# A 31-tap depthwise convolution: four channel tiles by 16-tap products through DRAM, two by 2-tap products, two on VectorE

## The reference, cut to what matters

```python
def conformer_conv(h, w_in, b_in, w_dw, b_dw, ln_g, ln_b, w_out, b_out):
    a, g = jnp.split(h @ w_in + b_in, 2, axis=-1)
    u = a * jax.nn.sigmoid(g)
    u = lax.conv_general_dilated(u, w_dw[:, None, :], window_strides=(1,),
        padding=[(CONV_WIDTH - 1, 0)], feature_group_count=D_MODEL) + b_dw   # width 31, per channel
    u = (u - mean(u)) * lax.rsqrt(var(u) + LN_EPS) * ln_g + ln_b             # over the channels
    return jax.nn.silu(u) @ w_out + b_out

def _rg_lru(...):
    a = jnp.exp(log_a)
    u = jnp.sqrt(-jnp.expm1(2.0 * log_a)) * (i * x)     # the recurrence's roots
    _, h = lax.associative_scan(_lin_combine, (a, u), axis=1)
```

## Time and profile before

| | |
|---|---|
| median of 3 runs | 2126.19 us (2125.86 to 2126.7) |
| the profiled execution | 2126.1 us, its span 2124.3 us |
| PE busy | 2084.4 us (98%) |
| PEld busy | 1861.9 us (88%) |
| DVE busy | 1596.5 us (75%) |
| ACT busy | 1230.8 us (58%) |
| POOL busy | 56.4 us (3%) |
| mean granted TensorE clock | 0.996 of full speed |

### The profile page before, as it was taken

The page is one execution under the profiler, slowest core; times in us unless marked ns, Lnnn a source line. Parts: engine busy times, 40 slices in busy tenths (PEclk is TensorE's granted clock), DMA queues, the critical chain, the costliest instruction groups (busy, mean ns, idle before and its releaser), DMA issues.

```text
span 2124.3 us, 39506 instructions
## 1 busy us (share of the span) xinstructions
PE 2084.4 (98%) x13412; PEld 1861.9 (88%) x13412; DVE 1596.5 (75%) x2804; ACT 1230.8 (58%) x2161; POOL 56.4 (3%) x78
## 2 busy tenths in 40 slices
PE   8999999999999999999999999999999999999998
PEld 8987889999999988878888888988888888888887
DVE  7687666999999975565557777878777777767776
ACT  4765455665667655445456556446556555656555
POOL 0020010000000000020000100000000000000000
PEclk9999999999999999999999999999999999999999
DMA  6442354555444455555555664315554555444554
GB/s 223 161 156 91 130 188 151 186 178 177 145 143 147 147 189 190 196 196 190 196 191 207 234 236 177 138 62 180 190 192 161 196 188 188 168 137 151 190 189 145
DMA packets 101114, 366.41 MB, mean 172 GB/s; under 512 B 11504, under 2 KB 12144, under 8 KB 100528
## 3 DMA queue, kind: packets, MB, share of 16 engines
q1 hardware_dynamic: 97776, 352.59, 47.9%
q0 software_dynamic: 3264, 12.85, 1.6%
HBM read 363.29 MB, written 2.10 MB: 172 GB/s over the span
## 4 chain that ended last, share of the span: by engine, by line
PE 91%; DVE 5%; ACT 3%; issue 1%; DMA 0%; DVEq 0%; ACTq 0%
PE acc L1785 16%; PE wide L2192 9%; PE wide L2193 9%; PE wide L2194 9%; PE acc L1790 8%; PE acc L1762 8%; PE acc L1763 8%; PE acc L1764 8%; PE wide L2178 2%; PE acc L2265 2%; DVE wlo L975 2%; PE sums L2025 1%; PE wide L1914 1%; PE wide L1915 1%; PE wide L1913 1%
## 5 line engine op out<-in xcount | busy, mean ns | idle before, releaser
L980 DVE TENSOR_TENSOR wlo<-raw,whi 128x1024 fp32r<-128x1024 f32 x396 | 488.6, 1234 | 205.8 <-ACT whi L463 200.7
L463 ACT ACTIVATE whi<-raw 128x1024 fp32r<-128x1024 f32 x450 | 475.3, 1056 | 228.8 <-PE wide L2194 226.8
L1762 PE MATMUL acc<-parts,whi 128*128 128x256 f32 (+1 forms) x1600 | 463.6, 290 | 2.9 <-DVE arena L1655 1.1
L1763 PE MATMUL acc<-parts,whi 128*128 128x256 f32 (+1 forms) x1600 | 454.1, 284 | 0.0
L1764 PE MATMUL acc<-parts,wlo 128*128 128x256 f32 (+1 forms) x1600 | 453.8, 284 | 0.0
L975 DVE TENSOR_TENSOR wlo<-raw,whi 128x1024 fp32r<-128x1024 f32 x268 | 327.9, 1225 | 105.2 <-ACT whi L458 93.3
L1785 PE MATMUL acc<-parts,whi 128*128 128x512 f32 x1504 | 374.9, 391 | 0.4 <-DVE arena L1726 0.4
L2192 PE MATMUL wide<-whi,small 128*128 128x512 f32 x896 | 350.5, 391 | 3.3 <-DVE small L1523 3.3
L2193 PE MATMUL wide<-whi,small 128*128 128x512 f32 x896 | 349.7, 390 | 0.0
L2194 PE MATMUL wide<-wlo,small 128*128 128x512 f32 x896 | 348.7, 389 | 0.0
L1785 PEld LDWEIGHTS acc<-parts,whi 128*128 128x128 f32 x1504 | 275.4, 188 | 53.5 <-issue 0.6
(11 more groups left out here) (351 smaller groups left out, 2353.4 us busy)
## 6 DMA issues: line engine op xcount, KB each, us to landing
raw<-stream SPq DMA_DIRECT2D x664, 512.0 KB, 3.2
arena<-taps_in POOLq DMA_DIRECT2D x20, 256.0 KB, 3.7
arena<-rows_in POOLq DMA_DIRECT2D x7, 512.0 KB, 4.1
arena<-h_in SPq DMA_DIRECT2D x2, 544.0 KB, 4.2
res<-rgw SPq DMA_DIRECT2D x1, 1024.0 KB, 8.3
res<-tokens_in POOLq DMA_DIRECT2D x1, 1024.0 KB, 5.1
park<-res POOLq DMA_DIRECT2D x1, 1024.0 KB, 4.1
res<-park POOLq DMA_DIRECT2D x1, 1024.0 KB, 6.2
```

The source lines that it names most:

```text
L463: act.activation(whi[:, c % RING, :], raw[:, c % RING, :], ACT.Copy).then_inc(hi_done, 1)
L980: V.tensor_tensor(wlo[:, c % RING, :], raw[:, c % RING, :], whi[:, c % RING, :].bitcast(F32), ALU.subtract).then_inc(lo_done, 1)
L1762: mm(out_, whi[:, s, w], xh, start=first, stop=False, **kw)
L1763: mm(out_, whi[:, s, w], xl, start=False, stop=False, **kw)
```

## The change

1. Tile 2 moves from DVE to PE. DVE keeps tiles 0 and 1 (62 taps). The gated tiles get two more zero columns at the end.
2. Tiles 2 to 5 take a new form, `quads`: POOL writes the gated tile to DRAM and loads it back four times, each time shifted by one more column, so that 128 partitions hold 32 channels at four shifts, for 4 groups of channels. One product then applies 16 taps (4 shifts times 4 output offsets), so a tile needs 4 groups x 2 products of 268 columns. ACT copies each group's result out of PSUM (`stage_out`), POOL writes it to DRAM and loads it back in four pieces so that the four offsets come to lie on the same partitions (`offsets_in`), and DVE adds the four pieces and the bias (`join`, three instructions). Tiles 6 and 7 keep the old form (`double`, `double_taps`, `part`, `join2`).
3. The products of tile 2 stand behind chunk 12 of `cin`, those of tile 3 behind chunk 14, those of tiles 4 and 5 behind chunk 15.
4. Diagonal weights: 16 DMAs instead of 20, under one semaphore. The load of the row `rows_of[6]` moves behind the new DMAs on POOL's queue.
5. `LN_ORDER` and the order of taps, joins and sums are written anew; DVE adds up tiles 0, 1 and 6.
6. The roots move from n = 7 and 11 to n = 9 and 12 of `uq`, behind the `split` of those steps, and a tanh of one element follows the second. In `uk`, DVE's `split` stands behind the copies of j = 1 and 5.

The diff, cut to its core:

```diff
-        DW_DVE, DW_PE = (0, 1, 2), (3, 4, 5, 6, 7)
+        DW_DVE, DW_QUADS, DW_DOUBLES = (0, 1), (2, 3, 4, 5), (6, 7)
+        QW, QN = 284, SEQ + 12
+        LN_ORDER = [("dw_joined", 1, 2), ("dw_joined", 2, 3), ("dw_dve", 1, 0), ("dw_dve", 2, 1),
+                    ("dw_joined", 4, 6), ("dw_joined", 5, 4), ("dw_joined", 7, 5), ("dw_joined", 8, 7)]
 # ACT, recurrence
-                if n in (7, 11):
-                    x = HR[:, n - 7:n - 3, :]
+                if n in (9, 12):
+                    x = HR[:, (n - 9) // 3 * 4:(n - 9) // 3 * 4 + 4, :]
                     act.wait_ge(sem("u_sq"), 1)
                     act.activation(x, x, ACT.Sqrt, scale=-0.25).then_inc(sem("u_root"), 1)
+                    if n == 12:
+                        act.activation(tiny[:, 62:63], tiny[:, 60:61], ACT.Tanh)
 # ACT, convolution
+            def stage_out(k):
+                if k >= 4:
+                    act.wait_ge(sem("offsets_out"), 16 * (k - 3))
+                for g in range(4):
+                    act.wait_ge(sem("dw_pe"), 4 * (k - 2) + g + 1)
+                    act.activation(staged(k)[:, g, :], wide[:, g, 0:QN], ACT.Copy).then_inc(sem("staged"), 1)
             for k in range(16):
...
+                if k in (13, 15):
+                    stage_out((k - 9) // 2)
+                if k == 14:
+                    double(0)
+                    double(1)
...
+            square(0)
+            stage_out(4)
+            double(2)
+            stage_out(5)
+            double(3)
+            split(BASE["cout"] + AHEAD)
+            square(1)
+            part(0)
+            part(1)
...
+            part(2)
+            part(3)
+            square(6)
+            square(7)
 # DVE
+            def join(k):
+                x = joined(k)
+                dve.wait_ge(sem(f"joined{k % 2}"), k // 2 * 64)
+                V.scalar_tensor_tensor(out=UC[:, k, :], in0=x[:, 0, :], scalar=v_("b_dw", k), in1=x[:, 1, :],
+                                       op0=ALU.add, op1=ALU.add)
+                link(V.tensor_tensor(x[:, 2, :], x[:, 2, :], x[:, 3, :], ALU.add))
+                V.tensor_tensor(UC[:, k, :], UC[:, k, :], x[:, 2, :], ALU.add).then_inc(sem("dw_joined"), 1)
             for k in range(16):
...
+                if k == 15:
+                    join(2)
                 if k % 2:
...
+                if 2 <= k <= 8:
+                    take_taps(2 * (k - 2), 2 * (k - 1))
+                if k >= 9:
+                    take_taps(14 + 3 * (k - 9), 14 + 3 * (k - 8))
+            take_taps(35, 48)
+            join(3)
+            take_taps(48, 62)
+            join2(0)
+            join2(1)
+            join(4)
...
+            join2(2)
+            join(5)
             split(BASE["cout"] + AHEAD)
+            join2(3)
 # PE
+            def quad_taps(k):
+                pe.wait_ge(sem("taps"), 16 * 16)
+                pe.wait_ge(sem("quads"), 64 * (3 if k < 5 else 4))
+                for g in range(4):
+                    if k > 2:
+                        pe.wait_ge(sem("staged"), 4 * (k - 3) + g + 1)
+                    for m in range(2):
+                        ins = mm(wide[:, g, 0:QN], DIAG[:, k - 2, g, m, :], quads(k)[:, g, 16 * m:16 * m + QN],
+                                 start=m == 0, stop=m == 1)
                     ins.then_inc(sem("dw_pe"), 1)
+            lin("cin", "mixpre0", after_pair=2, behind={12: (2,), 14: (3,), 15: (4, 5)})
+            double_taps(0)
+            double_taps(1)
+            for n in range(2):
+                pe.wait_ge(sem("csq"), n + 1)
+                ln_sums(UC[:, n + 2, :], sq(SEQ)[:, n + 2, :], n == 0, False)
+                double_taps(n + 2)
...
 # POOL
+            def shifted_in(k):
+                pool.wait_ge(sem("conv_in"), k + 1)
+                pool.dma_start(tiles_d[k - 2], UP[:, k, :]).then_inc(sem("tile_out"), 16)
+                pool.wait_ge(sem("tile_out"), 16 * (k - 1))
+                if k == 5:
+                    pool.wait_ge(sem("dw_pe"), 4)
+                for s in range(4):
+                    by_group = bass.AP(tiles_d.tensor, (k - 2) * P * (U + 2) + s, [[U + 2, 32], [32 * (U + 2), 4], [1, QW]])
+                    pool.dma_start(quads(k)[32 * s:32 * s + 32, :, :], by_group).then_inc(sem("quads"), 16)
+            def offsets_in(k):
+                pool.wait_ge(sem("staged"), 4 * (k - 1))
+                pool.dma_start(offsets_d[k - 2], staged(k).rearrange("p g n -> p (g n)")).then_inc(sem("offsets_out"), 16)
+                pool.wait_ge(sem("offsets_out"), 16 * (k - 1))
+                if k >= 4:
+                    pool.wait_ge(sem("dw_joined"), k - 3)
+                for g in range(4):
+                    by_offset = bass.AP(offsets_d.tensor, (k - 2) * P * 4 * QN + g * QN,
+                                        [[4 * QN, 32], [32 * 4 * QN + 4, 4], [1, SEQ]])
+                    pool.dma_start(joined(k)[32 * g:32 * g + 32, :, :], by_offset).then_inc(sem(f"joined{k % 2}"), 16)
+            for k in DW_QUADS:
+                shifted_in(k)
+            for k in DW_QUADS:
+                offsets_in(k)
```

More of the change, by code:

```diff
@@ L863, in _, with double, square @@
             in_root(2, None)
-            def double(k):
-                n = DW_PE.index(k)
+            def double(q):
+                k, c = 6 + q // 2, slice(64 * (q % 2), 64 * (q % 2) + 64)
                 act.wait_ge(sem("conv_in"), k + 1)
[L868 to L871, removed]
+                act.activation(doubled(q)[0:64, :], UP[c, k, 0:U], ACT.Copy).then_inc(sem("doubled"), 1)
+                act.activation(doubled(q)[64:128, 0:U - 1], UP[c, k, 1:U], ACT.Copy).then_inc(sem("doubled"), 1)
+            def stage_out(k):
[4 more added lines that the diff above has]
+                    act.activation(staged(k)[:, g, :], wide[:, g, 0:QN], ACT.Copy).then_inc(sem("staged"), 1)
+            def square(n):
+                by, count, k = LN_ORDER[n]
+                act.wait_ge(sem(by), count)
+                act.activation(sq(SEQ)[:, k, :], UC[:, k, :], ACT.Square).then_inc(sem("csq"), 1)
             for k in range(16):
@@ L881, in _ @@
                                    bias=v_("b_in", 8 + j)).then_inc(sem("cgate"), 1)
-                    if j - 1 in DW_PE:
-                        double(j - 1)
-            double(7)
             def part(q):
[L888 to L900, removed]
+                act.wait_ge(sem("dw_pe"), 16 + q + 1)
+                act.activation(parts_of[0:64, q, :], conv_bank(q)[64:128, OVER:OVER + SEQ], ACT.Copy).then_inc(sem("dw_part"), 1)
+            square(0)
[7 more added lines that the diff above has]
+            part(1)
+            square(2)
             square(3)
-            split(BASE["cout"] + AHEAD)
-            part(6)
-            part(7)
             square(4)
-            part(8)
             square(5)
-            part(9)
+            part(2)
+            part(3)
             square(6)
@@ L1228, in _ @@
                     V.tensor_copy(K1[0:64, 2 * j + 1, :], m[64:128, 0:T]).then_inc(outputs_read["V"], 1)
+                if j % 4 == 1:
+                    split(b + j // 4 + AHEAD)
             def scores(h):
@@ L1848, in turn_half, with lin @@
                     ins.then_inc(sem("turned"), 1)
-            def lin(stage, name, n=SEQ, after_pair=None):
+            def lin(stage, name, n=SEQ, after_pair=None, behind=None):
                 b, first = BASE[stage], 0
@@ L1875, in lin @@
                               (lambda: in_spread(after_pair)) if k == 2 and after_pair == 2 else None).then_inc(used, 1)
+                    if behind is not None and k in behind:
+                        for tile in behind[k]:
+                            quad_taps(tile)
                     if k == 0 and after_pair == ("cq", "ckv"):
```

142 lines of the change are left out of this document (67 added, 75 removed).

## The result

The changed kernel took 2132.28 us (median of ten runs, 2129.65 to 2133.74) against 2125.88 for the kernel before beside it (2123.93 to 2128.89): a ratio of 1.0032, interval 1.0024 to 1.0041. It is slower, by 6.4 us, 5 to 9 us by the interval. The forecast was 2115.1, faster, range to 2122.5; the result lies outside it and on the other side. It is within 0.1 us of the rival that I called "the round trips become the bound", to which I had given 0.07. The profiled execution has a span of 2130.9 us against 2124.3.

What follows compares the result with a forecast made beforehand. PE and DVE were taken to bound the convolution side by side. 9.3 us there plus 1.8 at the roots made 11.1, from 2126.1 to 2115.0, median 2115.1 us; range 2111 to 2122.5.

Steps and rivals of the forecast that it cites:

- the round trips become the bound: Rival: in the convolution, landings of 6.2 us let POOL's queue set the pace, slower than before: 2132.3 us; chance 0.07.
- PE's work: Convolution: a quad tile takes 3.66 us, all taps 29.5, 7.7 less; with sums, PE's work falls by 6.9 us.
- VectorE's and ScalarE's work: Convolution: DVE 11 us less, a new join 1.25, no longer the bound unless a join is late; ACT's balance nothing.
- The issue: POOL's DMAs in the convolution: each issue holds POOL for 0.54 us, bounds 0.54 and 1.5.
- The landings: Trips through DRAM: tile's write 3.0 us, products' write 3.9, loads 3.7; POOL needs 5.2 a tile, under 5.76.
- Step 1 of the timetable: Behind chunk 12: first quad product waits for twelve loads of tiles 2 to 4, landed 1354.4; PE waits 1.2 us.
- my timetable: Convolution: tile 5's products end at 1377.7, the last sums at 1397.8 against 1407.20, taken as 9.3 us earlier.
- Steps 3 and 4: Behind chunk 15: tile 2's pieces land at 1369.5, joined 1370.7; stage_out(4) from about 1372, tile 5's products not late.
- The roots: Stretch of the roots ahead of the attention: 1.8 us of PE's 2.66 us idle goes, bounds 0 and 2.7.

Runs made afterwards that it cites:

- the best version: Changed kernel with a semaphore per quad tile, join(2) and the squares moved later, and loads to 128 partitions each: 2110.99 us, 0.9934 of the kernel before.
- the probe: Kernel before with the new DMA patterns issued twice into unused memory, in a quiet place and beside the weight stream: 2126.31 us.

## Why the prediction was wrong, step by step

- **PE's work** held. A quad tile takes 3.62 to 3.78 us against 3.66. In the best version, whose PE waits for nothing of the new path, the taps take 29.4 us (four quad tiles and two of the old form), against 29.5.
- **VectorE's and ScalarE's work** held: a join is 0.40 + 0.45 + 0.35 = 1.2 us against 1.25, and VectorE is not the bound where the pieces are there.
- **The issue** held: 0.55 us against 0.54.
- **The landings are the step that failed**: "I take 3.0 for the tile's write, 3.9 for the products' write, 3.7 for every load. POOL then needs 5.2 us a tile, just under the 5.76". These are about right in a quiet place (3.1, 3.2, 3.6). Beside the stream the probe shows 5.6, 7.5 and 5.9, and the changed kernel itself 7.4 and 5.9 for the writes of tiles 3 and 4, 7.9 for a products' write, 6.9 and 7.0 for loads; the trips of tiles 3 and 4 held POOL for 9.6 and 8.1 us. I sized them from the medians of loads that came one at a time, though the earlier trace rows has one of 64 KB at 6.2 us and one of 512 KB at 7.4. And I looked for a crowd among the DMAs of before, where the change brings the crowd itself: twenty DMAs of 142 or 144 KB on the way out, on top of a stream that already held 0.53 of the DMA engines, and sixteen of 128 KB and four of 536 KB on the way back. The margin was 0.56 us a tile, and one late landing used it.
- **Step 1 of the timetable multiplied it.** I had seen that the first product waits for twelve loads, and priced it at 1.2 us from landings that were too short. It was 12.4. From `cin`'s start to the end of tile 5's products the kernel needs 18.6 us more than my timetable; 11.2 of them are this wait. Own semaphores are worth 9.6 us in the changed kernel, 10.8 in the best one.
- **A term was missing: the clock behind the wait.** I read the half clock at 1406 to 1408 behind a PE wait, and did not apply it to the waits that I added. The sixteen products behind the 12.4 us wait took 6.1 us and those behind the 3.3 us wait 5.4, instead of 3.66: 4.2 us together.
- **Steps 3 and 4 were right in place and wrong in size.** Pieces of tile 2 landed at 1385.7, where I had 1369.5 (18.4 us later, counted from `cin`'s start); `join(2)` stands on VectorE ahead of the last gating and `square(0)` on ScalarE ahead of `stage_out(4)`. I wrote that `stage_out` comes "while PE does tile 4", in time. It came 3.3 us late. Moving both is worth 7.2 us once the first wait is gone. 11.2 + 4.2 + 3.3 are 18.7 us, the whole of the 18.6.
- **The roots** held: 2.2 or 2.3 us by the start of `cin` in three pairs of traces, against 1.8 with bounds of 0 and 2.7. The times of whole executions (3.0 and 3.1 us) are too uncertain to say more.
- **The rival that came true** had the right mechanism, and its first instants. It counted from the kernel before, whose `cin` starts 2.2 us later; on that clock the measured ones are in brackets. With 6.2 us landings it put the first quads at 1365.4 (1365.6), tile 2's pieces at 1385.2 (1388.0), the end of tile 5's products at 1391.7 (1396.3) and the last sums at 1415.2 (1416.6). That its time, 2132.3, meets 2132.28 to 0.1 us is luck. It left out the clock (4.2 us) and took GpSimd's last trips as too slow: the last two writes, issued at 1389.6 and 1395.8 with nothing of the stream beside them, land after idle times of 3.45 and 3.51 us. It took 0.4 us less for the roots than they gave, and nothing for the 0.6 us gained behind the last sums. What failed was its chance. "Nothing shows such patterns" was an argument for width on both sides, and I had treated it as one for the median.
- VectorE's work beside GpSimd's DMAs was not the cause (the third theory, above).

Left open: what exactly the stream and the trips contend for (the DMA engines, their ports or DRAM), since no run kept the trips and slowed the stream; and which of the two moved instructions gave how much of the 7.2. That the broad loads are quicker because they reach more ports is the reading that fits, argued and not shown.

## What to carry to other kernels

A chain of small DMAs that runs beside a weight stream has to be sized from DMAs beside that stream, with its own ones added to the crowd: here the same transfers took 3.0 to 3.6 us in a quiet place and 3.6 to 7.5 in company, and a margin of 0.56 us a tile was no margin. Let each consumer wait for its own transfers: one counter for twelve loads cost about 10 us in two kernels. And put nothing that waits for such a trip ahead of work, on VectorE or ScalarE, that TensorE needs next; a wait of TensorE is to be priced with the half clock behind it, where it is long enough (3.3 us was, 1.4 us was not).

## What the runs showed of the hardware

- Four loads to 32 partitions and four to 128 of the same bytes differ little in a quiet place (3.6 and 3.0 us) and much beside the stream (5.9 and 3.6, in windows of 0.93 and 0.82 DMA share).
- A write of 144 KB with no other trip beside it took 2.7 us in the changed kernel and 3.7 in the probe, the stream moving in both. Behind four narrow loads and beside the stream it took 5.6 to 7.4 us, behind four in a quiet place 3.1.
- A write of 536 KB behind four loads took 7.9 us while 0.52 MB of the stream moved beside it, and 4.0 with nothing of the stream, at nearly the same mean share of the DMA engines (0.69 and 0.64).
- An issue of a DMA on GpSimd costs 0.54 to 0.57 us for one-level and three-level patterns alike.
- The granted clock falls to 0.50 (1.2 GHz) in a TensorE wait of 12.4 us, and sixteen products behind it then take 6.1 us instead of 3.7 to 3.8. Behind waits of 6.7, 6.8 and 7.2 us they took 6.8 to 6.9, behind 3.3 us 5.4, behind 1.4 us 3.85. So a longer wait doesn't cost more clock here.
